# Loading x by time step, building the S5 kernel K from E and raw C, and an earlier mix of the second tile, in a YOCO decoder step on one core

## The reference

```python
# layer 0: RMSNorm -> S5 mixer + GLU -> residual; RMSNorm -> PEER -> residual
bu = einsum('nlgj,gpj->nlgp', u, bb)            # 64 groups of 16 inputs, 64 complex states
h[t] = ab * h[t-1] + bu[t]                      # diagonal complex scan over time
y = re(einsum('nlgp,gjp->nlgj', h, c)) + d_skip * u
z = gelu(y);  zz = z @ w_glu;  out = zz[:, :1024] * sigmoid(zz[:, 1024:])
# PEER: per token 8 heads, product-key top 16 of 128 x 128 experts
a = gelu(x . u_tab[eid]) * softmax(scores);  out = sum(a * v_tab[eid])
# layer 1: RMSNorm -> windowed grouped-query attention -> residual; RMSNorm -> PEER -> residual
```

## Time and profile before

| what | value |
|---|---|
| median of 3 runs | 3443.28 us (3442.04 to 3449.44) |
| the profiled execution's own time | 3440.18 us |
| its span, first to last instruction | 3438.4 us |
| mean granted TensorE clock | 0.943 |
| busy: PE, VectorE, ScalarE, POOL | 2765.8, 2370.8, 940.8, 2307.6 us |
| bytes moved, mean rate | 1290.96 MB, 375 GB/s |
| of these gathers of expert rows | 1208.11 MB |

### The profile page before, as it was taken

How to read it: one execution, slowest core, us unless ns; L and a number is a source line. 1 busy time by engine, 2 the same in 40 slices (tenths; PEclk the granted TensorE clock), 3 DMA queues, 4 the chain that set the end, 5 groups by cost and what they waited for, 6 DMA issues and landing times.

```text
span 3438.4 us, 29178 instructions
## 1 busy us (share of the span) xinstructions
PE 2765.8 (80%) x7825; PEld 1310.0 (38%) x7825; DVE 2370.8 (69%) x5394; ACT 940.8 (27%) x2220; POOL 2307.6 (67%) x2331
## 2 busy tenths in 40 slices
PE   1597899967779888787787899887987878788776
PEld 1554443333335434333343445443343324333222
DVE  6836677767777776667777778767776666666663
ACT  4322222212232343212233225322222222222221
POOL 1116777767777677667777767677777677677774
PEclk9798999989889999998999999999999999999999
DMA  3348999999999999999999999999999999999997
GB/s 51 68 174 327 408 409 403 408 398 395 401 409 403 401 386 405 409 409 407 402 401 409 401 386 403 396 409 408 402 399 408 408 410 408 401 409 409 403 405 268
DMA packets 366817, 1290.96 MB, mean 375 GB/s; under 512 B 41832, under 2 KB 45544, under 8 KB 365432
## 3 DMA queue, kind: packets, MB, share of 16 engines
q0 software_dynamic: 331776, 1208.11, 89.1%
q1 hardware_dynamic: 34880, 80.99, 7.3%
HBM read 1283.21 MB, written 3.83 MB: 374 GB/s over the span
## 4 chain that ended last, share of the span: by engine, by line
DMA 33%; POOL 25%; PE 23%; issue 12%; DVE 4%; ACT 2%; SPq 1%; DVEq 0%; ACTq 0%; POOLq 0%
DMA arena<-in_peer_u,eid 16%; DMA arena<-in_peer_v,eid 15%; PE ps L1789 14%; POOL arena L2081 13%; POOL arena L2068 12%; PE ps L1718 2%; PE ps L1746 2%; DMA arena<-in_x 1%; PE ps L1894 1%; DVE arena L693 1%; DVE arena L1014 1%; PE ps L1846 1%; SPq L597 1%; DVE arena L984 1%; PE ps L1668 0%
## 5 line engine op out<-in xcount | busy, mean ns | idle before, releaser
L1789 PE MATMUL ps<-arena 128*128 128x512 f32 x4068 | 2054.9, 634 | 502.0 <-DMA arena<-in_peer_v,eid 357.0
L984 DVE CUSTOM_DVE_ANT_0 arena<-arena,ps 128x1024 f32<-128x1024 f32 x1058 | 1290.9, 1220 | 850.2 <-DMA arena<-in_peer_u,eid 834.4
L2081 POOL DMA_INDIRECT arena<-in_peer_v,eid x1152 | 1140.9, 990 | 517.5 <-issue 278.2
L2068 POOL DMA_INDIRECT arena<-in_peer_u,eid x1152 | 1139.4, 989 | 489.9 <-issue 304.0
L1789 PEld LDWEIGHTS ps<-arena 128*128 128x128 f32 x4068 | 756.1, 199 | 1535.0 <-issue 1079.4
L1366 ACT ACTIVATE arena<-ident,av 128x128 f32<-128x128 f32 x889 | 333.0, 397 | 858.5 <-PE ps L1789 766.9
L1746 PE MATMUL ps<-arena 128*128 128x256 f32 (+2 forms) x1088 | 288.2, 396 | 7.2 <-issue 2.7
L1746 PEld LDWEIGHTS ps<-arena 128*128 128x128 f32 x1088 | 204.0, 200 | 151.8 <-issue 123.2
L1006 DVE SCALAR_TENSOR_TENSOR arena<-arena,av 128x1024 f32<-128x1024 f32 x135 | 173.6, 1286 | 23.0 <-DMA arena<-in_peer_v,eid 17.4
L1337 ACT COPY arena<-ps 128x256 f32<-128x256 f32 x72 | 26.8, 373 | 495.9 <-PE ps L1774 495.9
L1718 PE MATMUL ps<-arena 128*128 128x512 f32 (+1 forms) x320 | 154.3, 603 | 0.8 <-ACT arena L566 0.8
(11 more groups left out here) (215 smaller groups left out, 1873.0 us busy)
## 6 DMA issues: line engine op xcount, KB each, us to landing
arena<-in_peer_wq SPq DMA_DIRECT2D x16, 2048.0 KB, 18.9
arena<-in_peer_u,eid POOLq DMA_INDIRECT x1152, 11.1
arena<-in_peer_v,eid POOLq DMA_INDIRECT x1152, 11.1
arena<-in_w_glu SPq DMA_DIRECT2D x2, 4096.0 KB, 13.9
arena<-in_w_q SPq DMA_DIRECT2D x2, 4096.0 KB, 32.1
arena<-in_w_o SPq DMA_DIRECT2D x2, 4096.0 KB, 26.1
arena<-in_keys SPq DMA_DIRECT2D x16, 256.0 KB, 20.8
arena<-in_x SPq DMA_DIRECT2D x10, 256.0 KB, 19.9
```

The source lines that it names most:

```text
L984: dve.tensor_tensor_reduce(UROWS[:, g % RING, :], UROWS[:, g % RING, :], x, 1.0, 0.0, ALU.mult, ALU.add, hp[:, j % 2, k:k + 1]).then_inc(d ...
L1789: mm = pe.matmul(ps[:, half, :], DIAG[:, (PE_DONE[j] + i) % 4, :], VROWS[:, g % RING, half * 512:(half + 1) * 512], start=(s.first and i = ...
L2068: pool.indirect_dma_start(UROWS[:, g % RING, :], None, io[f"peer_u{SLOT[j].layer}"], bass.IndirectOffsetOnAxis(ap=eid[:, j % 4, k:k + 1], ...
L2081: pool.indirect_dma_start(VROWS[:, g % RING, :], None, io[f"peer_v{SLOT[j].layer}"], bass.IndirectOffsetOnAxis(ap=eid[:, j % 4, k:k + 1], ...
```

## The change

Three things are changed.

- x is loaded by time step: one transfer of the sample chunks with its own semaphore, then eight transfers, one for each step, of 64 rows of 4 KB. ScalarE squares step s when its transfer is in.
- K is not built from CA any more. The product of E with a block-diagonal copy of raw C (CPAIR: two groups side by side, the imaginary part negated) gives the block row of K for the last step, with all eight lags, in one go; two copies bring it to SBUF. POOL adds the skip term to its last 32 rows, and SP places the other seven block rows by transfers that shift it to lower partitions. Before that POOL clears CPAIR, the places of K's first four block rows and, later, parts of the others. ScalarE waits for the first clearing before it writes CPAIR. K, Z, SKIP, CRAW change places in the area; the second half of w_glu now also waits for Z to be turned.
- VectorE's mix of the second tile moves from steps 9, 11 and 13 of slot 0 to steps 1, 2 and 4, and ScalarE's part from step 15 to step 3.

The diff, cut to its core:

```diff
-        M = area(0, Q, G, GS)
-        Z = area(0, Q, D)
+        Z = area(12800, Q, D)
-        K = area(12800, Q, G, GS)
+        K = area(0, Q, G, GS)
-        CRAW = area(0, 2, PAIRS, GS)
+        CRAW = area(5 * D, 2, PAIRS, GS)
+        CPAIR = area(6 * D, 2, PAIRS, 2 * GS)
...
@@ SP
-            chunks = io["x"][0:SEQ, :].rearrange("(a i s) d -> i a (s d)", i=Q, s=Q)
-            for i in range(Q):
-                sp.dma_start(arena[Q * i:Q * i + Q, 0:Q * D], chunks[i]).then_inc(x_in, 16)
-            sp.dma_start(arena[CH:NC, 0:Q * D], io["x"][SEQ:TOK, :].rearrange("(c s) d -> c (s d)", s=Q)).then_inc(x_in, 16)
+            sp.dma_start(X[CH:NC], io["x"][SEQ:TOK, :].rearrange("(c s) d -> c s d", s=Q)).then_inc(sample_in, 16)
+            chunks = io["x"][0:SEQ, :].rearrange("(a i s) d -> s i a d", i=Q, s=Q)
+            for s in range(Q):
+                sp.dma_start(X[0:CH, s, :], chunks[s]).then_inc(x_in[s], 16)
...
-            sp.wait_ge(zeroed, 1)
             sp.wait_ge(skip_added, 1)
-            for s in range(Q):
-                sp.dma_start(K[GS * s:GS * s + GS, s:Q, :, :], M[0:GS, 0:Q - s, :, :]).then_inc(k_in, 16)
+            for n, t in enumerate((0, 1, 2, 3, 4, 6, 5)):
+                sp.wait_ge(zeroed, max(n - 2, 1))
+                sp.dma_start(K[0:GS * (t + 1), t], K[P - GS * (t + 1):P, Q - 1]).then_inc(k_in, 16)
...
             sp.wait_ge(y_ready, PR)
+            sp.wait_ge(z_ready, 2 * KT)
             sp.dma_start(WGLU[:, 0:4, :], glu[:, 4:8, :]).then_inc(glu_late_in, 16)
@@ VectorE, first_slot
-                if k == 9:
+                if k == 1:
                     mix_whole(1)
-                if k == 11:
+                if k == 2:
                     mean_square(1)
-                if k == 13:
+                if k == 4:
                     refine(1)
                     normalise(1)
@@ ScalarE
-            act.wait_ge(x_in, 16 * (Q + 1))
+            act.wait_ge(sample_in, 16)
             for s in range(Q):
+                act.wait_ge(x_in[s], 16)
                 c(act.activation(SQ[0:NC, :], X[0:NC, s, :], ACT.Square, accum_out=st[0:NC, 0, s:s + 1]))
...
             act.activation(CA[:, 1, :, 0, :], CRAW[:, 1], ACT.Copy, scale=-1.0).then_inc(ends_copied, 1)
+            act.wait_ge(zeroed, 1)
+            for ri in range(2):
+                for g2 in range(2):
+                    rows = slice(SD * g2, SD * g2 + SD)
+                    act.activation(CPAIR[rows, ri, :, GS * g2:GS * g2 + GS], CRAW[rows, ri], ACT.Copy,
+                                   scale=-1.0 if ri else 1.0).then_inc(c_paired, 1)
             for r, (ri, q0) in enumerate(WR):
                 turned_copy(NU + r, WIN[:, q0:q0 + 4, :, ri, :],
...
-            for r in range(PR):
-                act.wait_ge(turned, NU + NW + r + 1)
-                for g2 in range(2):
-                    act.copy(M[0:GS, :, 8 * r + g2:8 * r + 8:2, :], ...
-            act.wait_ge(k_in, 16 * Q)
+            act.wait_ge(k_ready, 1)
+            for half in range(2):
+                act.copy(K[:, Q - 1, half * PAIRS:(half + 1) * PAIRS, :],
+                         ps[:, 4 + half, :].rearrange("p (g j) -> p g j", j=GS)).then_inc(k_copied, 1)
...
-                if k == 15 and j == 0:
+                if k == 3 and j == 0:
                     root(1)
                     xt_copy(1)
@@ PE
-            pe.wait_ge(ca_ready, 2)
-            pe.wait_ge(ends_copied, 4)
+            pe.wait_ge(c_paired, 4)
             pe.wait_ge(v_act, 4 * len(VR))
...
+            for q in range(PAIRS):
+                out = ps[:, 4 + q // 16, q % 16 * 2 * GS:(q % 16 + 1) * 2 * GS]
+                for ri in range(2):
+                    mm = pe.matmul(out, E[:, ri, q, :], CPAIR[:, ri, q, :], start=(ri == 0), stop=(ri == 1))
+            mm.then_inc(k_ready, 1)
+            pe.wait_ge(k_in, 16 * (Q - 1))
+            pe.wait_ge(k_copied, 2)
@@ POOL
+            c(pool.memset(dsk[P - 2 * GS:P, :], 0.0))
+            c(pool.memset(dskip_gain[P - 2 * GS:P, :], 0.0))
+            pool.nop().then_inc(skip_cleared, 1)
             pool.wait_ge(powers_ready, 1)
             pool.wait_ge(bb_ready, 1)
...
             pool.nop().then_inc(carries_ready, 1)
 
-            pool.wait_ge(turned, NU + NW)
-            pool.memset(K[:, 0:Q - 1], 0.0).then_inc(zeroed, 1)
+            pool.wait_ge(normed, Q)
+            c(pool.memset(CPAIR, 0.0))
+            c(pool.memset(K[:, 0:4], 0.0))
+            pool.nop().then_inc(zeroed, 1)
...
+            pool.wait_ge(k_copied, 2)
+            c(pool.tensor_tensor(K[low, Q - 1], K[low, Q - 1], SKIP, ALU.add))
+            pool.nop().then_inc(skip_added, 1)
+            c(pool.memset(K[SD:P, 4], 0.0))
+            pool.nop().then_inc(zeroed, 1)
+            c(pool.memset(K[low, 6], 0.0))
+            pool.nop().then_inc(zeroed, 1)
+            pool.wait_ge(ca_ready, 2)
+            c(pool.memset(K[low, 5], 0.0))
+            pool.nop().then_inc(zeroed, 1)
```

More of the change, by code:

```diff
@@ L348, in build @@
         TMP = area(38400, PAIRS * BLK)
-        SKIP = area(12800 + (Q - 1) * D, G, GS)[0:GS]
+        SKIP = area(4 * D, G, GS)[P - 2 * GS:P]
         CARRY = area(20992, 2, 2, PAIRS, CH // Q)
@@ L438, in build @@
         hf = part(2, PAIRS)
-        dsk = part(G)[0:GS]
-        dskip_gain = part(G)[0:GS]
+        dsk = part(G)
+        dskip_gain = part(G)
         consts = part(2)
@@ L445, in build @@
         ps = ctx.enter_context(nc.psum_tensor("ps", [P, 8, 512], F32))
-        x_in, gain_in, par_in = sem("x_in"), sem("gain_in"), sem("par_in")
+        gain_in, par_in, sample_in = sem("gain_in"), sem("par_in"), sem("sample_in")
+        x_in = [sem(f"x_in{s}") for s in range(Q)]
         bc_in, ident_in = sem("bc_in"), sem("ident_in")
@@ L454, in build @@
         spread, bb_ready, carries_ready = sem("spread"), sem("bb_ready"), sem("carries_ready")
-        ends_copied, glu_late_in = sem("ends_copied"), sem("glu_late_in")
+        ends_copied, glu_late_in, c_paired = sem("ends_copied"), sem("glu_late_in"), sem("c_paired")
+        skip_cleared, k_copied = sem("skip_cleared"), sem("k_copied")
         powers_ready, s_pool = sem("powers_ready"), sem("s_pool")
         turned, turned_out = sem("turned"), sem("turned_out")
-        skip_added, k_in = sem("skip_added"), sem("k_in")
+        skip_added, k_in, k_ready = sem("skip_added"), sem("k_in"), sem("k_ready")
         v_ready, v_act = sem("v_ready"), sem("v_act")
@@ L580, in _ @@
             sp.dma_start(BRAW, io["s5b"]).then_inc(b_in, 16)
-            chunks = io["x"][0:SEQ, :].rearrange("(a i s) d -> i a (s d)", i=Q, s=Q)
-            for i in range(Q):
-                sp.dma_start(arena[Q * i:Q * i + Q, 0:Q * D], chunks[i]).then_inc(x_in, 16)
-            sp.dma_start(arena[CH:NC, 0:Q * D], io["x"][SEQ:TOK, :].rearrange("(c s) d -> c (s d)", s=Q)).then_inc(x_in, 16)
+            sp.dma_start(X[CH:NC], io["x"][SEQ:TOK, :].rearrange("(c s) d -> c s d", s=Q)).then_inc(sample_in, 16)
+            chunks = io["x"][0:SEQ, :].rearrange("(a i s) d -> s i a d", i=Q, s=Q)
+            for s in range(Q):
+                sp.dma_start(X[0:CH, s, :], chunks[s]).then_inc(x_in[s], 16)
             sp.dma_start(ident[:, :], io["ident"]).then_inc(ident_in, 16)
             sp.dma_start(h0[:, :, :, :], io["h0"]).then_inc(bc_in, 16)
-            sp.dma_start(dsk[:, :], io["dskip"]).then_inc(bc_in, 16)
-            sp.dma_start(dskip_gain[:, :], io["gains"][0, :].rearrange("(g j) -> j g", j=GS),
+            sp.wait_ge(skip_cleared, 1)
+            sp.dma_start(dsk[P - GS:P, :], io["dskip"]).then_inc(bc_in, 16)
+            sp.dma_start(dskip_gain[P - GS:P, :], io["gains"][0, :].rearrange("(g j) -> j g", j=GS),
                          allow_slow_non_contiguous=True).then_inc(skip_gain_in, 16)
@@ L1271, in _ @@
                         v_copy(act.copy, r, pairs, ri, g2).then_inc(v_act, 1)
-            for r in range(PR):
-                act.wait_ge(turned, NU + NW + r + 1)
-                for g2 in range(2):
-                    act.copy(M[0:GS, :, 8 * r + g2:8 * r + 8:2, :],
-                             ps[0:GS, 4 + 2 * (r % 2) + g2, :].rearrange("p (q l j) -> p l q j", q=4, j=GS))\
-                       .then_inc(turned_out, 1)
-            act.wait_ge(k_in, 16 * Q)
+            act.wait_ge(k_ready, 1)
+            for half in range(2):
+                act.copy(K[:, Q - 1, half * PAIRS:(half + 1) * PAIRS, :],
+                         ps[:, 4 + half, :].rearrange("p (g j) -> p g j", j=GS)).then_inc(k_copied, 1)
             def z_copies(kt):
@@ L1695, in _ @@
             pe.wait_ge(scanned, 1)
+            pe.wait_ge(ca_ready, 2)
+            pe.wait_ge(ends_copied, 4)
             for r in range(PR):
@@ L2055, in _ @@
             pool.wait_ge(skip_gain_in, 16)
[L2056 to L2060, removed]
+            low = slice(P - 2 * GS, P)
+            c(pool.tensor_tensor(dsk[low], dsk[low], dskip_gain[low], ALU.mult))
```

(4 more changed lines are left out.)

## The result

The changed kernel takes 3463.05 us (median of four, 3461.24 to 3471.65) against 3444.05 us for the kernel before beside it: ratio 1.0065, 95% interval [1.005, 1.008]. Run again later it took 3461.05 us (3460.21 to 3475.25), ratio 1.0058 [1.004, 1.0076]. So it is slower by some 18 us. I had forecast 3455 us, some 12 above the runs shown then, with 3463 as the top of the range.

The account below looks back on a forecast made before the run. DMA's stream of expert rows bounds the kernel; only its start, about 305 us, can move. +11.6 - 0.6 + 2.0 - 0.7 = +12.3 on 3440.18 gives 3452.5; runs' median 3.1 above, so 3455 us, range 3422 to 3463.

Parts of the forecast that it names:

- x early: VectorE's wait for the squares of x: squares end near 25 us, all 22.48 us of waiting go, by itself -22.5 us.
- POOL held: POOL's 18 carry operations pass about one per end of a VectorE instruction; carries ready at 83 us instead of 41.
- Rival 1: POOL's carry operations get through, done by 51 us, in time for ScalarE: -21.7, so 3421.6 us; chance 0.20.
- V and the scan: Behind POOL's clearing and WIN's copies, V's last copy comes at 117.3 us; scan starts there instead of 105.74: +11.6 us.
- K: K's new products (7.3 us) and transfers (20 us) stay hidden behind the scan, 11 us to spare: -0.6 us.
- +2.0 for a cold PE: PE stands still before the output products and starts them at the lower clock: +2.0 us, bounds 0 and 3.8.
- w_glu: Second half of w_glu issued at most two rounds later while PE has gate products to do: 0 us (0 to 3.8).
- The second tile: Slot 0's earlier mix: query weights fetched 3.8 us earlier, PE's wait for them gone, softmax later: net -0.7 us (-4 to +3).
- Shared ports: VectorE and POOL on SBUF: by the skill's page VectorE would lose some 5 us more; forecast took about 1 us of holds.

Follow-up runs that it names:

- second profile: Profiled execution of the changed kernel run again unaltered, an ordinary one: 3460.93 us; median of that run 3461.05 us, ratio 1.0058 to the kernel before.
- first profile: Profiled execution of the changed kernel's first measurement, the longest of its runs: 3471.65 us, against a median of 3463.05 us.
- CPAIR late: Changed kernel with ScalarE's wait for the clearing and its four CPAIR copies moved behind the copies of V: 3433.05 us, ratio 0.9973 to the kernel before.
- early clearing: Changed kernel with POOL's first clearing moved between the first and second doubling of the carries: 3432.93 us, ratio 0.9964 to the kernel before.
- mix in the middle: Kernel before with the second tile's mix at steps 7, 8 and 10, ScalarE's part at 9: 3445.93 us, ratio 1.001 to the kernel before.
- x alone: Kernel before with x loaded by time step and nothing else: 3430.31 us, ratio 0.9953 to the kernel before.

## Why the prediction was right, and where it failed

**x early**: right. The squares end at 28.5 (25 forecast); all 22.48 us of wait go.

**POOL held**: right, and the centre of it. One operation for each end of a VectorE instruction, the 18 done at 83.92 (83 forecast), `zeroed` at 89.5 (88.4), ScalarE's hole 32.73 us, WIN's last copy ending at 101.2 (100.3). Rival 1 is out: the operations did not get through. VectorE lost nothing that shows by letting them in (CA ended at 80.84 in the second profile, 81.7 forecast). What I left unsaid is that this price hangs on one wait's place: moving POOL's clearing or ScalarE's wait gives 28 to 30 us back.

**V and the scan**: +11.6 forecast, +12.9 measured in the second profile. In the first V fell to the lower clock, 10.9 us more; I had bounds for PE's transposes and its output products, and none for V.

**K**: hidden, but not as sized. Its products were to take 7.3 us (4 to 15) and took 27.5 (second profile):

```profile
118.69 27.49 PE L1670 MATMUL ps<-arena 128*128 128x32 f32 x128 [2.60 <-ACT arena L559]
```

I had halved V's 128 of the earlier trace rows because the program has 64 products for K. But it has 64 for V too, and the profile shows both as 128, so nothing was to be halved; and K's ran at granted clock 0.50, 0.21 us each. The seven transfers were to take 20 us and took 11.3 (159.67 to 170.92, first profile). Instead of 11 us to spare, 1.81 us were left in which PE waited for the scan. K decides only in CPAIR late, where its products start late; in early clearing the output products still waited 5.15 us for the scan. The +2.0 for a cold PE did not come: the first 64 output products took 3.77 us, as in the earlier trace rows, behind within-chunk products just done.

**w_glu**: 0, as forecast; no wait for it is seen ahead of the gate products or in them.

**The second tile** is the step that failed: "SP fetches the next query weights 3.8 us earlier, and PE's 2.71 us wait for them goes. Net -0.7 us". The fetch did start some 4 us earlier against the gate products (7.4 us later than before, with the gate products 11.6 later), and VectorE stood at the second and the thirteenth dot as foreseen. But I asked only when the load starts, and took it to last as long as before, 8.8 us. The earlier mix brings the load forward and holds gathers back, by the stand and, as the mix in the middle shows, without it too; they run beside the load, and with the keys it takes 21.6 us. That made +7.9 instead of -0.7, from +11.6 at the gate products to +19.5 at slot 1's queries. With 8.6 us more the forecast would have been 3463.6.

**Shared ports**: The Trainium skill, "SBUF — State Buffer", section "Who interferes with whom", says that a VectorE copy can enter a two-port mode, in which VectorE and GpSimd exclude each other, and that an operation with two SBUF inputs contends with GpSimd's reads and not with a GpSimd operation that only writes. The runs agree with both: in x alone the scan's copy took 6.37 us beside POOL's memset (the profile does not name the copy's mode), and the products of CA in the earlier trace rows took 4.44 us each, the first of them begun beside a memset.

## What to carry to other kernels

Before a wait is taken out, list what the other engines do in it, and whose waits stand behind that work: here an idle VectorE was what let POOL's small operations through, and the cure was to put the wait for POOL where it holds nothing else. A transfer that starts earlier need not land earlier, if it then shares DMA with what had been over before it; ask what the stand of an engine stops upstream of it, and what work pushed behind the moved piece was to release. When a profiled execution is the longest of its runs, take a second profile before reading a cause from it.

## What the runs showed of the hardware

TensorE stayed at a granted clock of 0.50, 1.2 GHz of 2.4, through 21.00 us in which it was busy for 21.00, with float32 matmuls of 72 columns. It had come to 1.00 over the transposes just before (from 0.50, between 94 and 100 us) and fell within these products; the same program ran them at 1.00 in another execution. K's products of 32 columns took 25.9 to 27.5 us in every profile of a kernel with the new K, at 0.50 but for at most their first two microseconds. The Trainium skill, "TensorE: Matmul & The Clock Gate", Part 1, ties the clock to how busy PE has been; these rows are not told apart by that. Why one execution falls and another does not stays open, as does whether the hole among the transposes has to do with it.
